# Heads 0 to 3 of the gated DeltaNet normed, gated and turned inside the fourth round of its core, and their half of the output product put behind the round

## The reference, cut to what matters

```
o_fwd = gated_delta_chunked(qh, kh, vh, gh[0], bh[0])
o_bwd = flip(gated_delta_chunked(flip(qh), flip(kh), flip(vh), ...))
o = transpose(o_fwd + o_bwd)                      # (B, S, H, DV)
o = o * rsqrt(mean(o * o, axis=-1, keepdims=True) + RMS_EPS)
o = o * norm_w * silu(z)
y = o.reshape(B, S, H * DV) @ w_out               # 1024 x 1024
...
x = x + y
h = rmsnorm(x, norm_mlp[0]);  x = x + square(relu(h @ w1)) @ w2
```

## Time and profile before

| what | value |
|---|---|
| median of three runs | 2628.5 us (2626.69 to 2628.72) |
| the profiled execution | 2633.75 us, span 2631.2 us |
| busy, share of the span | PE 79%, PEld 52%, DVE 30%, ACT 21%, POOL 1% |
| granted TensorE clock, mean of the span | 0.902 |
| fourth round, first matmul to last add | 312.5 to 366.5 us |
| its end to the output product's first matmul | 366.5 to 384.1 us |
| output product | 384.1 to 414.9 us |

### The profile page before, as it was taken

How to read it: one execution, slowest core, us unless ns; L and a number is a source line. 1 busy time by engine, 2 the same in 40 slices (tenths; PEclk the granted TensorE clock), 3 DMA queues, 4 the chain that set the end, 5 groups by cost and what they waited for, 6 DMA issues and landing times.

```text
span 2631.2 us, 33285 instructions
## 1 busy us (share of the span) xinstructions
PE 2090.2 (79%) x13800; PEld 1370.7 (52%) x13800; DVE 789.9 (30%) x1509; ACT 541.4 (21%) x946; POOL 31.6 (1%) x49
## 2 busy tenths in 40 slices
PE   7877668998988997999886666665999977666665
PEld 6656445886755885777542222222777742222221
DVE  4543453566554574122220000002122130000002
ACT  3221133441124442042110000001033110000000
POOL 0000000000000000000000000000000000000000
PEclk9978879998998998999978888887999978888887
DMA  8200013765954675432339999999332419999997
GB/s 299 99 1 34 2 65 128 255 251 175 378 207 160 227 266 174 145 128 97 160 125 426 427 426 427 425 427 383 130 128 72 184 73 427 426 426 427 427 426 293
DMA packets 150294, 641.69 MB, mean 244 GB/s; under 512 B 9310, under 2 KB 30840, under 8 KB 117046
## 3 DMA queue, kind: packets, MB, share of 16 engines
q1 hardware_dynamic: 143898, 637.13, 61.1%
q10 hardware_dynamic: 6300, 3.20, 0.4%
HBM read 639.21 MB, written 1.10 MB: 243 GB/s over the span
## 4 chain that ended last, share of the span: by engine, by line
PE 57%; DMA 30%; DVE 6%; issue 3%; ACT 2%; DVEq 1%; POOL 1%; SPq 0%; ACTq 0%; POOLq 0%
DMA ring<-in_w_down 30%; PE psum L1149 6%; PE psum L807 5%; PE psum L808 5%; PE psum L809 5%; PE psum L1265 3%; PE psum L1063 3%; PE psum L785 3%; PE psum L1052 3%; PE psum L905 2%; PE psum L599 2%; PE psum L1142 2%; PE psum L1225 1%; PE psum L630 1%; PE psum L922 1%
## 5 line engine op out<-in xcount | busy, mean ns | idle before, releaser
L1245 PE MATMUL psum<-ring,arena 128*32 128x256 f32 x4096 | 295.0, 439 | 188.1 <-DMA ring<-in_w_up 146.4
L1245 PEld LDWEIGHTS psum<-ring,arena 128*32 128x32 f32 x4096 | 141.6, 122 | 344.2 <-issue 146.1
L1265 PE MATMUL psum<-ring,arena 128*32 128x512 f32 x1024 | 164.8, 776 | 93.6 <-DMA ring<-in_w_down 84.4
L807 PE MATMUL psum<-arena_r 128*128 128x512 f32 x512 | 208.0, 406 | 14.7 <-DVE h_featmajor_r L1319 7.6
L809 PE MATMUL psum<-ring_r,arena_r 128*128 128x512 f32 x512 | 205.3, 401 | 0.0
L1904 DVE TENSOR_TENSOR arena<-psum,arena 128x256 f32<-128x256 f32 x32 | 13.6, 425 | 564.0 <-PE psum L1245 564.0
L1149 PE MATMUL psum<-h_featmajor,ring 128*128 128x256 f32 x768 | 173.6, 379 | 0.0
L1345 DVE TENSOR_TENSOR ring_r<-ring,arena_r 128x2048 fp32r<-128x2048 f32 x64 | 143.7, 2286 | 86.2 <-ACT arena_r L1962 86.1
L1149 PEld LDWEIGHTS psum<-h_featmajor,ring 128*128 128x128 f32 x768 | 145.9, 190 | 19.9
L2282 ACT ACT_TABLE_LOAD x32 | 41.1, 1283 | 523.0 <-PE psum L1245 523.0
L1962 ACT CAST arena_r<-ring 128x2048 fp32r<-128x2048 f32 x64 | 119.6, 1904 | 71.1 <-PE psum L809 71.1
(11 more groups left out here) (358 smaller groups left out, 2595.6 us busy)
## 6 DMA issues: line engine op xcount, KB each, us to landing
ring<-in_w_gate SPq DMA_DIRECT2D x64, 2048.0 KB, 26.6
ring<-in_w_up SPq DMA_DIRECT2D x64, 2048.0 KB, 26.2
ring<-in_w_down SPq DMA_DIRECT2D x64, 2048.0 KB, 26.3
ring<-in_mlp_w SPq DMA_DIRECT2D x32, 2048.0 KB, 7.9
ring<-in_w_mod SPq DMA_DIRECT2D x24, 2048.0 KB, 11.5
ring<-in_w_in SPq DMA_DIRECT2D x20, 2048.0 KB, 8.2
ring<-in_gdn_w_in SPq DMA_DIRECT2D x8, 2048.0 KB, 17.8
ring<-in_dswa_w_in SPq DMA_DIRECT2D x9, 1536.0 KB, 14.9
```

The costliest lines, as they stand in the source:

```text
L807: mm(o, xh, wh, start=start, stop=False, skip_group_check=True)
L1245: ins = mm(PS[32 * j:32 * j + 32, 4 + m, 0:T], XGE[:, 4 * u + kk, :], W(v + 2 * m + u, D)[:, kk, j * T:(j + 1) * T], start=u == 0 and kk = ...
L1265: ins = mm(PS[32 * j:32 * j + 32, (7, 4)[half], :], HTE[:, k % 2, 32 * (k // 2):32 * (k // 2) + 32], W(v + 4 + u, D)[:, j, half * 512:(hal ...
```

## The change

It does the norm, gate and turning in two parts of four heads. On VectorE norm_sums(0) (squares and sums of heads 0 to 3) goes between the expansion L1505 and the masked copies L1510 of round 3, gated(0) between L1510 and L1513. ScalarE's table switch and silus of the first half of Z go ahead of its expansion L2030. GpSimd's power is done twice, 8 columns each. TensorE turns heads 0 to 3 between L751 and L756 into banks 4 and 5, ScalarE copies them into the place of Z's first half, and the product of U_GOUT (16 matmuls with Z as lhs) stands right behind L766, bank by bank. Then come the second half's eight transposes, one copy each on ScalarE and VectorE, and `rows_product` for U_GOUT + 1. The number of matmuls, transposes and DMAs stays; the order of loads in SyncE's queue too. XN[:, 1] holds the first half's y, since the small tiles use XN[:, 0]. z_act's counts shift: 4 and 5 are now the first silus.

```diff
--- before.py
+++ after.py
@@ -365,7 +365,9 @@
         ajunk = sb("act_junk", [P, 1])
         eps = sb("eps", [P, 1])
         JUNK = lanes[0]["DT"][:, 0]
-        GJUNK = ar[:, GJ:GJ + 2048]
+        GJUNK = ar[:, GJ:GJ + 1024].rearrange("p (t h e) -> p t h e", t=TT, e=P)
+        YA = XN[:, 1, :].rearrange("p (t n) -> p t n", t=TT)
+        YB = XN[:, 0, :].rearrange("p (t n) -> p t n", t=TT)
         MSTAGE = ar[:, GJ + 512:GJ + 512 + NMASK]
         w_full = [sem(f"w_full{i}") for i in range(RING)]
         w_free = [sem(f"w_free{i}") for i in range(RING)]
@@ -751,6 +753,12 @@
                     ins = mm(pair(2, P)[:, h], lanes[fst]["KD"][:, h, 1], VN[:, h], start=True, stop=True)
                 ins.then_inc(sem("tail_mm"), 1)
 
+                if it == 3:
+                    for t in range(TT):
+                        pe.wait_ge(sem("y_ready"), t + 1)
+                        for dc in range(4):
+                            ins = nc.tensor.transpose(pair(4 + t, P)[:, dc], YA[:, t, dc * P:(dc + 1) * P], ident)
+                    ins.then_inc(sem("y_turned"), 1)
                 pe.wait_ge(sem("s_out"), it + 1)
                 for h in range(4):
                     mm(pair(0, P)[:, h], KQT[:, hg + h, 0, snd * P:(snd + 1) * P], SST[:, h], start=True, stop=True)
@@ -767,11 +775,22 @@
                 ins.then_inc(sem("tail_mm"), 1)
 
 
-            pe.wait_ge(sem("z_act"), 4)
+            full(pe, U_GOUT)
+            pe.wait_ge(sem("y_back"), 2)
+            for b in range(4):
+                t, h = b // 2, b % 2
+                if b == 1:
+                    pe.wait_ge(sem("core_done"), 4)
+                if b == 3:
+                    pe.wait_ge(sem("z_act"), 6)
+                for kk in range(4):
+                    ins = mm(bank(b), Z[:, t, kk * P:(kk + 1) * P], W(U_GOUT, D)[:, kk, h * 512:(h + 1) * 512],
+                             start=kk == 0, stop=False, skip_group_check=True)
+            used(ins, U_GOUT)
             for t in range(TT):
-                pe.wait_ge(sem("y_ready"), t + 1)
-                for dc in range(KC):
-                    ins = nc.tensor.transpose(pair(3 + dc // 2, P)[:, (dc % 2) * 2 + t], XN[:, t, dc * P:(dc + 1) * P], ident)
+                pe.wait_ge(sem("y_ready"), 2 + t + 1)
+                for dc in range(4):
+                    ins = nc.tensor.transpose(pair(4 + t, P)[:, dc], YB[:, t, dc * P:(dc + 1) * P], ident)
             ins.then_inc(sem("y_turned"), 1)
             pe.wait_ge(sem("y_back"), 4)
 
@@ -788,8 +807,7 @@
                         ins.then_inc(sem("half_mm"), 1)
                 used(ins, n)
 
-            for u in range(2):
-                rows_product(U_GOUT + u, 0, HT[:, 4 * u:4 * u + 4, :], u == 0, u == 1)
+            rows_product(U_GOUT + 1, 0, HT[:, 4:8, :], False, True)
             if stop == "gdn":
                 return
 
@@ -1459,6 +1477,38 @@
             v.tensor_tensor(flat(KD_S), PS[:, 7, 32:64], flat(GC), ALU.subtract).then_inc(sem("decay_in"), 1)
             dve.wait_ge(sem("decay_out"), 1 + 1)
 
+            by_head = lambda a: a.rearrange("p (t h) -> p t h", h=GH)
+            rq, so, pw, fac = (by_head(SPT[:, i, 0:16]) for i in range(4))
+
+            def norm_sums(u, scratch):
+
+                hs4 = slice(4 * u, 4 * u + 4)
+                o = O_ACC[:, :, hs4]
+                v.tensor_tensor(scratch, o, o, ALU.mult)
+                v.tensor_scalar(rq[:, :, hs4], RQV[:, :, hs4], P ** -0.5, None, ALU.mult)
+                settle()
+                v.tensor_reduce(so[:, :, hs4], scratch, AX, ALU.add)
+                for _ in range(2):
+                    settle()
+                    v.tensor_tensor(so[:, :, hs4], so[:, :, hs4], rq[:, :, hs4], ALU.mult)
+                settle()
+                v.tensor_scalar(so[:, :, hs4], so[:, :, hs4], 1.0 / P, EPS, ALU.mult, ALU.add).then_inc(sem("gdn_ms"), 1)
+
+            def gated(u, y):
+
+                hs4 = slice(4 * u, 4 * u + 4)
+                for t in range(TT):
+                    dve.wait_ge(sem("z_act"), 3 * u + 3 + t + 1)
+                    z = Z[:, t, u * 512:(u + 1) * 512].rearrange("p (a b) -> p a b", b=P)
+                    v.tensor_tensor(z, z, bm(NW, 4), ALU.mult).then_inc(sem("tok_out"), 1)
+                dve.wait_ge(sem("gdn_rs"), 1 + u + 1)
+                v.tensor_tensor(fac[:, :, hs4], pw[:, :, hs4], rq[:, :, hs4], ALU.mult)
+                settle()
+                for t in range(TT):
+                    v.tensor_tensor(y[:, t].rearrange("p (h e) -> p h e", e=P), O_ACC[:, t, hs4], bc(fac[:, t, hs4], P), ALU.mult)
+                    settle()
+                    v.tensor_tensor(y[:, t], y[:, t], Z[:, t, u * 512:(u + 1) * 512], ALU.mult).then_inc(sem("y_ready"), 1)
+
             masks = marks[:, 0:2 * 7 * P].rearrange("p (w s i) -> p w s i", w=2, s=7)
             masks32 = marks[:, 2 * 7 * P:NMASK].rearrange("p (w s i) -> p w s i", w=2, s=NSMALL + 1)
             for it in range(4):
@@ -1505,9 +1555,13 @@
                         ins = v.tensor_copy(lanes[l]["Tm"][r, :, r], small[l]["Tm"][r])
                     ins.then_inc(sem("expanded"), 1)
                 settle()
+                if it == 3:
+                    norm_sums(0, YA.rearrange("p t (h e) -> p t h e", e=P))
                 for l in range(2):
                     dve.wait_ge(sem("q_mm"), (it * 5 + NSMALL) * 2 + l + 1)
                     v.copy_predicated(lanes[l]["Tm"], bm(masks[:, d, NSMALL + 1], 4), pair(4 * l + 1, P)).then_inc(sem("t_grown"), 1)
+                if it == 3:
+                    gated(0, YA)
                 for l in range(2):
                     dve.wait_ge(sem("r_mm"), it * 2 + l + 1)
                     v.copy_predicated(lanes[l]["U"], bm(masks[:, 1 - d, nlev_], 4), pair(4 * l + 2, P)).then_inc(sem("u_grown"), 1)
@@ -1538,34 +1592,10 @@
                     v.tensor_tensor(o, o, qs, ALU.add).then_inc(sem("core_done"), 1)
 
             settle()
-            oa = O_ACC.rearrange("p t h e -> p (t h e)")
-            v.tensor_tensor(GJUNK, oa, oa, ALU.mult)
-            settle()
-            rq, so, pw, fac = s2[0].rearrange("p a b -> p (a b)"), s2[1].rearrange("p a b -> p (a b)"), SPT[:, 2, :], SPT[:, 3, :]
-            v.tensor_reduce(so[:, 0:16], GJUNK.rearrange("p (a e) -> p a e", e=P), AX, ALU.add)
-            v.tensor_scalar(rq[:, 0:16].rearrange("p (t h) -> p t h", h=8), RQV[:, :, 0:8], P ** -0.5, None, ALU.mult)
-            settle()
-            v.tensor_tensor(so[:, 0:16], so[:, 0:16], rq[:, 0:16], ALU.mult)
-            settle()
-            v.tensor_tensor(so[:, 0:16], so[:, 0:16], rq[:, 0:16], ALU.mult)
-            settle()
-            v.tensor_scalar(so[:, 0:16], so[:, 0:16], 1.0 / P, EPS, ALU.mult, ALU.add).then_inc(sem("gdn_ms"), 1)
-            for u in range(2):
-                for t in range(TT):
-                    dve.wait_ge(sem("z_act"), 4 + 2 * u + t + 1)
-                    z = Z[:, t, u * 512:(u + 1) * 512].rearrange("p (a b) -> p a b", b=P)
-                    v.tensor_tensor(z, z, bm(NW, 4), ALU.mult).then_inc(sem("tok_out"), 1)
-            dve.wait_ge(sem("gdn_rs"), 1 + 1)
-            v.tensor_tensor(fac[:, 0:16], pw[:, 0:16], rq[:, 0:16], ALU.mult)
-            settle()
-            for t in range(TT):
-                y = XN[:, t, :].rearrange("p (h e) -> p h e", e=P)
-                v.tensor_tensor(y, O_ACC[:, t], bc(fac[:, t * 8:(t + 1) * 8], P), ALU.mult)
-                settle()
-                v.tensor_tensor(XN[:, t, :], XN[:, t, :], Z[:, t, :], ALU.mult).then_inc(sem("y_ready"), 1)
-            dve.wait_ge(sem("y_turned"), 1)
-            for i in (2, 3):
-                v.tensor_copy(HT[:, 2 * i:2 * i + 2, :], pair(3 + i, T)).then_inc(sem("y_back"), 1)
+            norm_sums(1, GJUNK)
+            gated(1, YB)
+            dve.wait_ge(sem("y_turned"), 2)
+            v.tensor_copy(HT[:, 4:8, P:T], pair(5, P)).then_inc(sem("y_back"), 1)
             low(0, 0)
             low(0, 1)
             residual(1, lambda: spent(dve, U_GOUT + 1))
@@ -2023,6 +2053,10 @@
                     for l in range(2):
                         act.wait_ge(sem("p_mm"), (it * nlev_ + q) * 2 + l + 1)
                         a.copy(small[l]["PP"].rearrange("p h c -> p (h c)"), PS[:, 4 * l, 0:P]).then_inc(sem("p_out"), 1)
+                if it == 3:
+                    for t in range(TT):
+                        z = Z[:, t, 0:512]
+                        a.activation(z, z, ACT.Silu).then_inc(sem("z_act"), 1)
                 act.wait_ge(sem("cleared"), it + 1)
                 for l in range(2):
                     act.wait_ge(sem("u_grown"), (it * nlev_ + NSMALL - 1) * 2 + l + 1)
@@ -2043,6 +2077,10 @@
                     if i == 0:
                         act.wait_ge(sem("tail_mm"), 6 * it + 2)
                         a.copy(SST, pair(7, P)).then_inc(sem("s_out"), 1)
+                        if it == 3:
+                            act.wait_ge(sem("y_turned"), 1)
```

(20 more changed lines are left out.)

## The result

The changed kernel takes 2609.86 us (median of 5 runs, 2607.94 to 2615.95) against 2627.68 us (2626.18 to 2628.72): 17.8 us less, ratio 0.9936 with a 95% interval of 0.9922 to 0.9951. Two later timings of the same code gave 0.9929 (0.9916 to 0.9943) and 0.9926 (0.9912 to 0.9939). By the medians these are 19.8 and 20.2 us. The forecast was 2610.5 us, 18.0 less than the median shown then.

The account below looks back on a forecast made before the run. VectorE's norm and gate left TensorE empty before a slow-clocked product. Core 1.7 us later, product end 18.9 earlier, 0.9 lost at the residual: 18.0 off median 2628.5 gives 2610.5 us, range 2606.5 to 2616.

Parts of the forecast that it names:

- What bounds the stretch: Core's end to MLP: VectorE's norm and gate leave TensorE empty 13 us; the product then loses 3.2 us to slow clock.
- Part 1: VectorE in round four: norm_sums(0) costs 0.1 us; with gated(0), L742 starts 0.8 us later.
- Part 2: ScalarE in round four: table load and two silus take 2.4 us, L2030 0.5 late, within 0.9 slack, cost 0.
- Part 3: TensorE in the tail: eight more transposes between L751 and L756 make the core 0.9 us later, whole.
- Part 4: Output product moved up behind the core, VectorE ready 2 to 4 us early: product ends 18.9 us earlier.
- Part 5: MLP start: VectorE's low halves delay the residual, 0.9 of 18.9 us lost, so L807 starts 18.0 us earlier.
- The sum: L807, the MLP's first matmul, starts 18.0 us earlier; subtracted from the median 2628.5, this gives 2610.5 us.
- (a): Rival: VectorE's round costs 1 to 3 us more, by the power and hand-overs; 2611.5 to 2613.5 us, chance 0.12.
- (b): Rival: ScalarE's switch to silu costs twice 1.30 us, silus end 0.4 past the slack; 2610.9 us, chance 0.03.
- (c): Rival: the clock drops in the product's first half anyway and gives 3.2 us back; 2613.7 us, chance 0.1.
- (d): Rival: the earlier product is hidden, a transfer or VectorE's weight work paces the MLP; 2628.5 us or part, chance 0.04.
- (e): Rival: slower, the clock stays at 1.2 GHz through the whole product; 2638 us, chance 0.02.

Follow-up runs that it names:

- e1_norm_only: Changed kernel with the output product not moved: all 64 records run together after the second half's y is copied; median 2622.9 us, ratio 0.9973.
- b1_before: The kernel before the change, unaltered, profiled and timed again; median 2631.26 us, ratio 1.0001.
- e2_no_round_work: Changed kernel without round four's norm, gate, silus, transposes and copies of heads 0 to 3; median 2614.99 us, ratio interval 0.9918 to 0.9954.
- e3: Kernel before, plus twelve unused matmuls in the hole between core and y transposes; 2633.57 us, ratio 1.0018; repeated 2635.03 us, 1.0013.
- v4: Changed kernel with round-four additions moved into idle times, the residual ahead of the last low half, and five unused matmuls per round; 2610.48 us, 0.9932.

## Why the prediction was right, step by step

- **What bounds the stretch** (VectorE's turn, TensorE empty, the product behind it): right. With VectorE's half of the work moved but TensorE's not, 6.6 us come; with the product moved too, 12.2 more.
- **Part 1, VectorE in round four**: mis-sized, 0.8 us taken, 0.10 us measured without the spell and 0.04 with it. In e1_norm_only, without the spell, the copies behind norm_sums(0) start 0.2 us earlier in the round than summed, and the masked copies, which I had put at 0.73 to 0.75 us each, take 1.33 a pair when nothing separates them. gated(0) itself took 348.21 − 343.96 = 4.25 us, against 4.3. L744 starts 11.98 us behind the expansion copy; L742 did 11.88. With the spell VectorE waits 1.2 us for TensorE before L1562; from there gated(0) and the copies L1567 carry the changed kernel's chain, and L744 starts 13.59 us behind the expansion copy, against 13.55 in b1_before and e2_no_round_work.
- **Part 2, ScalarE and the table**: right. The silu starts 336.15 − 334.86 = 1.29 us behind the start of the load, and the expansion L2064 begins 0.4 us late, within its slack. The drain of some 1.38 us that the Trainium skill ("ScalarE: Activation LUTs", What ACT_TABLE_LOAD costs) adds to a switch is not seen here either.
- **Part 3, the transposes**: right, 0.87 of 0.9 us, whole. Parts 1 to 3 together: 0.9 for 1.7.
- **Part 4, the product**: right. From its start to its end 392.23 − 362.84 = 29.4 (forecast 29.2), at a clock of 1.00, VectorE 3.5 us ahead of it. From its end to L825 4.0 (forecast 4.2), of which TensorE waits 1.2 for the normed half (forecast 1.5).
- **Part 5, what is late next**: right in kind and nearly in size: the low halves and the residual end last, and taking them away gives 0.66 of 0.9.
- **The sum**: 18.0 forecast for the stretch, 18.9 at equal clock. The 0.9 between them are 0.8 of parts 1 to 3 and 0.2 of part 5, less 0.2 by which part 4 was too short. That the raw profiles show 17.2 is the spell, which the profile of before had missed and which is worth 1.67 there. The medians came out 17.8, 19.8 and 20.2 us lower on three occasions; that the first of them is within 0.2 us of the forecast is luck, since a repeat moves by up to 2.4 us.
- **The rivals**: (a) and (b), a dearer round, did not come: it was cheaper. The price of (b), and the 0.5 us in part 2 beside it, were worked out wrongly: the slack of 0.9 us counts from L2030's old start, 341.54, and not from 342.0, so silus that end at 343.3 would be 0.9 us past it and not 0.4. Nothing else rests on that. (c) to (e): the clock held at 1.00, and what was won was kept: behind L807 the changed kernel takes 2211.6 to 2212.0 us in its three profiles, the kernel before 2213.0 and 2209.6. The clock's share of the gain, 3.2 us by my row, wasn't had by filling with twelve matmuls (1.3 us in the product, 2.2 with the transposes); in the changed kernel both halves of the product run at the full rate.

## What to carry to other kernels

A product that is a sum over heads can start with the heads that are ready; here two thirds of the gain came from putting TensorE's work into the hole, one third from shortening the vector work that made it. When an engine's idle times are filled, cost pairs of short instructions back to back (1.33 us for two) and not by their isolated rows (0.73 each with a wait between), and look at a spell of slow clock too: it can hold up the other engine and hide part of what was filled in (0.04 us here, 0.10 without it). And compare profiles from one landmark to another at the same clock: here 6 of the 23 us between two spans were no part of the change.

## What the runs showed of the hardware that I had not expected

- The same instructions of rounds one to three took 166.0 to 174.0 us in thirteen profiles, at a mean granted clock of 0.90 in the shortest and 0.85 in the longest; in round four the first 16 records of L716 or L718 took 2.10 us without a spell of slow clock and 2.67 to 3.02 with one.
- A hole filled with matmuls did not keep the clock up behind the thin work that followed: 0.59 at the start of the product in e3, where no wait since the filling was longer than 1.4 us, and 0.69 and 0.61 in the small blocks of v4, where a wait of 3.2 us was left.
- The kernel before with its hole filled was slower as a whole by 0.18 and 0.13% in two timings, although the filled stretch was 2.2 us shorter; the cause is open.
- A higher granted clock did not shorten the rounds by what was forecast: 0.95 over rounds one to three in v4, and 167.1 us, where 0.90 went with 166.0 in the changed kernel.
